# Two decoder blocks on one core: every projection with the tokens stationary, and strips turned by a trip through device memory

## The chip, the cores and the metric

The kernel runs on one core of a Trainium2 chip. The metric is device time in microseconds, from one execution of the whole program. Three runs of the kernel before gave 2118.93, 2119.08 and 2119.95 us; the median, 2119.08 us, is the time before. The profile is of one further execution, whose span from first to last instruction is 2117.7 us.

Engine names in the rows: PE is TensorE's matmuls, PEld its loads of the stationary operand, DVE is VectorE, ACT is ScalarE, POOL is GpSimd, SP is SyncE, whose queue (SPq) issues most DMAs.

## The reference

256 tokens of 2048 features go through two blocks, in float32.

```python
# block one
a = rms_norm(h, norm_mix)
q, k, v = split(a @ sb_w_qkv)                     # 16 heads of 128
A = exp(log_sigmoid(z) + sum of -softplus(z) of the keys between)   # z = q k / sqrt(128), keys before the query
h = h + (A @ v) @ sb_w_o
h = h + square(relu(rms_norm(h, norm_mlp) @ mlp_w1)) @ mlp_w2      # 8192 hidden
x = rms_norm(h, final_norm)
# block two
z = rms_norm(x, pre_mix_g) @ w_in                 # q, k, v: 8 heads of 128; u: 1024 for the pool
a = softmax attention over chunks, with a bias by distance
p = (trailing means of u over 2, 4, 8, 16 tokens, less u) @ pool_w, per group of 256, times pool_scale
x = x + rms_norm(concat(a, p) @ w_o, post_mix_g)
up = causal_dwconv(rms_norm(x, pre_ffn_g) @ w_up)  # 3 taps over tokens, 2 x 5632
y = (gelu(up[:, :5632]) * up[:, 5632:]) @ w_down
out = x + rms_norm(y, post_ffn_g)
```

## The kernel before

**Pieces and strips.** The program is one list of 746 pieces. A piece is 256 rows by 512 columns of some weight matrix (512 KB); 8, 10 or 12 pieces make a strip of 512 output columns. Each weight and each activation is split into a high half, rounded for the fast float32 matmul (fp32r), and the rest as a low half; a product is high x high + high x low + low x high. The split of piece i is an ACT copy into `Wh` (L930) and a DVE subtraction into `Wl` (L1146). There are 6 raw buffers (`NRAW`) and 5 split buffers (`NW`), and the split of piece i+4 stands in the program ahead of PE's products of piece i.

**Two kinds of piece.** In kind "N" the tokens are stationary (`row_products`, 12 matmuls of 512 columns) and the result has tokens as partitions, in two banks of PSUM. In kind "T" the weights are stationary and the tokens, high and low side by side, are moving:

```python
for m in range(4):
    c = slice(t * 512 + m * 128, t * 512 + (m + 1) * 128)
    mm(P[:, m, :], wh[:, c], x, ...)                  # 512 columns: x high and x low
    r = mm(P[:, m, 0:TOK], wl[:, c], x[:, 0:TOK], ...)  # 256 columns
```

That is 8 matmuls of 512 columns and 8 of 256 a piece; the result has features as partitions, in four banks, and its two halves have to be added. What needs features as partitions is of kind T: q and k of both attentions, w1 of the MLP, the pool's u, and w_up. These are 52 strips of 8 pieces, 416 pieces. v, w_o, w2 and w_down are of kind N, 328 pieces. Two pieces of `pool_w` have a kind of their own with the columns of T.

**Evacuation of a T strip.** ACT copies the low half (`low_copy`, L900), DVE adds it to the high half (`low_add`, L1104) into `T1`. For q and k DVE scales by the norm's factor, which lies as a row over all partitions (`r_a`, `r_b`; L1201); for w_up and the pool POOL does it (L1482, L1464); for w1 DVE squares (L1272), ACT and DVE make the halves (L1020, L1275). The factor gets into a row by a `spread`: a diagonal matrix on DVE (L1121), a float32 matmul with ones, a copy on ACT (L982).

**PSUM.** There are two sets of four banks. Strips use them in turn, and side work (scores, weights, values, norms, turned tiles) uses the set that the running strip does not (`side_set`).

**Order.** `plan_program` walks through the pieces. For each it emits the splits that are due, the products, at a strip's last piece the evacuation, and then the jobs that were put down for this piece by `after(i, job)` and `later(n, job)`. Each engine gets its part of the steps in that one order, and waits only on semaphores. So a job's place says behind which split and before which split each engine meets it. With v the first piece of a group's v strip, the scores come after piece v+1, the attention weights after v+8, the values after v+12.

**Trips through device memory** exist for eight strips of rows: after w_o of block one, after the last w2 strips and once for w_up. SP writes the rows (L856, two DMAs of 256 KB), waits for them, reads them back in four DMAs of 128 KB as 32-token blocks (L861), and DVE transposes 32x32 blocks (L1242). The softmax's probabilities take a similar trip (L865, L868, L1339).

Of the kernel before, what the change touches and what calls it, by code (L numbers as in the profile page):

```python
# [4 lines left out]
F32 = mybir.dt.float32  # L5
# [47 lines left out]
def plan_program(sem):  # L53
    p = Plan(sem)
    step, done, after, later = p.step, p.done, p.after, p.later
    free = {n: [] for n in ("QK1", "T0", "T1", "E", "zs", "set0", "set1", "mT", "qk0", "qk1", "v0", "v1", "A0", "A1")}
# [3 lines left out]
    def side_set():  # L60
        return 1 - now[0]
# [13 lines left out]
    tile_hl = [None] * KT  # L75

# [7 lines left out]
    def strip(w, col, ks, mov, tiles, evac, kind="T", koff=0):  # L84
        first = len(p.pieces)
        for n, kp in enumerate(ks):
            src = (w, "rows", kp * 256, col)
            p.pieces.append(dict(src=src, shape=2, mov=mov, kt=2 * (kp - koff), tiles=tiles, kind=kind, first=n == 0,
                                 last=n == len(ks) - 1, evac=evac, wide=False, early=None))
        return first  # L90
# [12 lines left out]
    def rms(name, col):  # L103
# [3 lines left out]
        r, diag = done("rms_r"), done("rms_diag")  # L107
        step("rms", set=s, col=col, need=st["total"], free=list(free[f"set{s}"]), ones=ones0, ident=ident,
             total=total, mean=mean, root=root, rec=rec, sq=sq, prod=prod, r=r, diag=diag)
        free["zs"], free[f"set{s}"] = [total], [mean]  # L110
        st[name + "c"] = r
        st["diag"] = diag
# [8 lines left out]
    def row_norm(squared=False, spreads=None):  # L121
# [3 lines left out]
        kw = dict(square=done("rms_r")) if squared else dict(square=None)  # L125
        if spreads:
            kw.update(diag=done("rms_diag"), ident=ident, zs_free=list(free["zs"]))
        step("row_norm", need=st["rows_sq"], total=total, mean=mean, root=root, rec=rec, sq=sq, prod=prod, r=r, spreads=spreads, **kw)
        if squared:
            st["r2sq"] = kw["square"]  # L130
        if spreads:
            st["diag"] = kw["diag"]
            after(p.at + 2, lambda: spread(spreads, "r_b"), ahead=True)

    def row_pair():
# [5 lines left out]
        both, diag = done("rms_r"), done("rms_diag")  # L141
        step("row_pair", need=st["rows_sq"], zs_free=list(free["zs"]), ident=ident, total=total, mean=mean, first=first,
             square=square, moved=moved, mean2=mean2, second=second, both=both, diag=diag)
# [185 lines left out]
    for c, n in enumerate((6, 5, 5)):  # L329
        for j in range(n):  # L330
# [3 lines left out]
            if j == 0:  # L334
                p.pieces[i]["wide"] = True
# [1406 lines left out]
```

## Time and profile before

| | |
|---|---|
| median of 3 runs | 2119.08 us |
| span of the profiled execution | 2117.7 us (the median is 1.4 us above it) |
| PE busy | 2110.5 us, 10990 matmul records |
| PEld busy | 1810.4 us |
| DVE busy | 1259.2 us (59%) |
| ACT busy | 1049.5 us (50%) |
| POOL busy | 189.2 us (9%) |
| DMA | 415.11 MB, 61.3% of 16 engines on SP's queue |

Matmuls overlap in the records, so a mean of 390 ns is the life of one matmul, from its start to its end; what a stream of them costs is read from start to start. A float32 matmul that is not of the fast kind shows as two records.

### The profile page before, as it was taken

The numbers are of one execution on the slowest core, as the hardware profiler recorded it, in microseconds if no ns is written. First come the engines' busy times: TensorE is split into PE (matmuls) and PEld (weight loads), VectorE is DVE, ScalarE is ACT, GpSimd is POOL, SyncE is SP. The second block draws the span as 40 slices with busy tenths as digits, with TensorE's granted clock in tenths as the row PEclk, the third lists the DMA queues.
The fourth block names the chain that finished last, engine by engine and source line by source line (L and its number), as shares of the span: only waits on it lengthen the run. The fifth ranks groups of instructions, "written<-read, shape, count | busy, mean of one in ns | idle before, by whom it ended". The sixth has DMA issues, their size and how long they took to land.

```text
span 2117.7 us, 26776 instructions
## 1 busy us (share of the span) xinstructions
PE 2110.5 (100%) x10990; PEld 1810.4 (85%) x10990; DVE 1259.2 (59%) x1341; ACT 1049.5 (50%) x1222; POOL 189.2 (9%) x90
## 2 busy tenths in 40 slices
PE   9999999999999999999999999999999999999998
PEld 8888888888888888888888888888888888888887
DVE  6555656656455555465667755576666644566565
ACT  7554555544334443344555635465455443455543
POOL 3000000000000000000004000002222100222210
PEclk9999999999999999999999999999999999999999
DMA  8565557765666666666676567655655666556663
GB/s 289 171 207 172 180 169 232 223 195 174 209 193 183 199 211 191 186 193 195 219 238 189 178 210 228 195 183 173 195 191 178 217 191 192 182 175 199 204 210 120
DMA packets 220363, 415.11 MB, mean 196 GB/s; under 512 B 13521, under 2 KB 23889, under 8 KB 219729
## 3 DMA queue, kind: packets, MB, share of 16 engines
q1 hardware_dynamic: 219376, 408.92, 61.3%
q10 hardware_dynamic: 864, 4.49, 0.6%
q8 instruction: 86, 1.41, 0.3%
q14 instruction: 37, 0.30, 0.0%
HBM read 405.49 MB, written 7.86 MB: 195 GB/s over the span
## 4 chain that ended last, share of the span: by engine, by line
PE 100%; ACT 0%; DVE 0%; issue 0%; POOL 0%; DVEq 0%; POOLq 0%
PE ps L1503 99%; PE ps L1506 0%; ACT T L1075 0%; DVE QK L1390 0%; ACT raw L1088 0%; ACT aHL L954 0%; ACT zs L1085 0%; DVE rs L1407 0%; POOL ones L1434 0%; ACT rs L1080 0%; POOL ident L1432 0%; DVE rs L1404 0%; DVE rs L1409 0%; DVE rs L1399 0%; POOL tri L1433 0%
## 5 line engine op out<-in xcount | busy, mean ns | idle before, releaser
L1146 DVE TENSOR_TENSOR Wl<-raw,Wh 128x1024 fp32r<-128x1024 f32 x743 | 911.8, 1246 | 640.6 <-ACT Wh L930 639.9
L1503 PE MATMUL ps<-aHL,Wh 128*128 128x512 f32 x3336 | 1158.7, 392 | 0.5 <-ACT aHL L954 0.4
L930 ACT ACTIVATE Wh<-raw 128x1024 fp32r<-128x1024 f32 x743 | 767.6, 1054 | 588.9 <-PE ps L1503 585.4
L1503 PE MATMUL ps<-aHL,Wl 128*128 128x256 f32 x3328 | 929.3, 279 | 0.0
L1503 PEld LDWEIGHTS ps<-aHL,Wh 128*128 128x128 f32 x3336 | 624.2, 187 | 139.5 <-issue 0.9
L1503 PEld LDWEIGHTS ps<-aHL,Wl 128*128 128x128 f32 x3328 | 628.2, 189 | 0.5
L1503 PE MATMUL ps<-Wh,hid 128*128 128x512 f32 x1728 | 533.1, 389 | 0.0
L1503 PEld LDWEIGHTS ps<-Wh,hid 128*128 128x128 f32 x1728 | 324.4, 188 | 67.5
L1503 PE MATMUL ps<-Wl,hid 128*128 128x512 f32 x864 | 336.2, 389 | 0.0
L1503 PEld LDWEIGHTS ps<-Wl,hid 128*128 128x128 f32 x864 | 162.2, 188 | 33.5
L1503 PE MATMUL ps<-Wh,oHL 128*128 128x512 f32 x512 | 158.7, 389 | 0.0
L1482 POOL TENSOR_TENSOR T<-T,r_b 128x1024 f32<-128x1024 f32 x22 | 71.2, 3235 | 645.4 <-DVE T L1104 391.1
L1503 PE MATMUL ps<-Wh,aHL 128*128 128x512 f32 x384 | 121.1, 391 | 0.0
L1503 PEld LDWEIGHTS ps<-Wh,oHL 128*128 128x128 f32 x512 | 96.1, 188 | 20.1
L1503 PE MATMUL ps<-Wl,oHL 128*128 128x512 f32 x256 | 99.6, 389 | 0.0
L1104 DVE TENSOR_TENSOR T<-ps,T 128x1024 f32<-128x1024 f32 x54 | 66.0, 1223 | 54.8 <-ACT T L900 54.8
L900 ACT ACTIVATE T<-ps 128x1024 f32<-128x1024 f32 x54 | 55.3, 1024 | 69.1 <-PE ps L1503 69.1
L1503 PEld LDWEIGHTS ps<-Wh,aHL 128*128 128x128 f32 x384 | 72.1, 188 | 15.0
L1464 POOL TENSOR_TENSOR E<-T,r_b 128x1024 f32<-128x1024 f32 x2 | 7.0, 3486 | 825.7 <-DVE T L1104 813.2
L1503 PE MATMUL ps<-Wl,aHL 128*128 128x512 f32 x192 | 74.7, 389 | 0.0
L1486 POOL TENSOR_TENSOR E<-E,zs 128x1024 f32<-128x1024 f32 x11 | 49.0, 4455 | 95.6 <-DVE E L1366 95.6
L1503 PEld LDWEIGHTS ps<-Wl,oHL 128*128 128x128 f32 x256 | 48.1, 188 | 9.7
(175 smaller groups left out, 792.2 us busy)
## 6 DMA issues: line engine op xcount, KB each, us to landing
raw<-in_mlp_w_dram SPq DMA_DIRECT2D x256, 512.0 KB, 4.3
raw<-in_w_up_dram SPq DMA_DIRECT2D x176, 512.0 KB, 3.9
raw<-in_sb_w_qkv_dram SPq DMA_DIRECT2D x93, 512.0 KB, 4.8
raw<-in_w_down_dram SPq DMA_DIRECT2D x88, 512.0 KB, 4.2
raw<-in_w_in_dram SPq DMA_DIRECT2D x64, 512.0 KB, 4.4
raw<-in_sb_w_o_dram SPq DMA_DIRECT2D x32, 512.0 KB, 5.3
raw<-in_w_o_dram SPq DMA_DIRECT2D x32, 512.0 KB, 4.3
passed_rows<-xN SPq DMA_DIRECT2D x16, 256.0 KB, 4.3
```

The source lines that it names most:

```text
L900: e.activation(T0[:, :, :], ps[st["set"]][:, :, TOK:2 * TOK], ACT.Copy).then_inc(st["copied"][0], 1)
L930: e.activation(Wh[:, i % NW, :], rawv[:, i % NRAW, :], ACT.Copy).then_inc(st["hi"][0], 1)
L1104: e.tensor_tensor(T1[:, :, :], ps[st["set"]][:, :, 0:TOK], T0[:, :, :], ALU.add).then_inc(st["summed"][0], 1)
L1146: e.tensor_tensor(Wl[:, i % NW, :], rawv[:, i % NRAW, :], Wh[:, i % NW, :].bitcast(F32), ALU.subtract).then_inc(st["lo"][0], 1)
L1464: e.tensor_tensor(E4, T1[:, :, :], rows4("r_b"), ALU.mult).then_inc(st["scaled"][0], 1)
L1482: e.tensor_tensor(T1[:, :, :], T1[:, :, :], rows4("r_b"), ALU.mult).then_inc(st["done"][0], 1)
L1486: e.tensor_tensor(E4, E4, Z4, ALU.mult).then_inc(st["done"][0], 1)
L1503: return e.matmul(o, l, r, start=start, stop=stop, skip_group_check=True)
```

## The change

- Every projection piece but the two of the pool is of kind "N". A strip takes two banks of PSUM. Sets 0 and 1 have two banks each and are used by the strips in turn; set 2 has four banks and is the side set, and the pool pieces use it too.
- A strip that needs features as partitions makes a trip. ACT copies its two banks to `T0` with the norm's factor as a scale per partition (tokens are partitions now), or with relu and then a square (`stage_rows`). SP writes `T0` out as two DMAs; two pieces later it waits for them and reads back as four (`land_rows`); two pieces after that DVE transposes the 32x32 blocks into the place wanted (`turn_strip`). One trip is under way at a time; another waits in a list. Columns within each group of 128 of these weights are permuted on the host to fit the blocks.
- Low copies, sums and scalings of such strips go, and with them `spread`, `diagonal`, `r_a`, `r_b`, and the matmul on `r_a` that opened four strips.
- Scores, attention weights and values stand three pieces later (v+4, v+11, v+15), for the first group two more.
- The strips of w_o in both blocks and of w_down are paired: with a tail of 2, the first pair's strips run all but their last two pieces, then these.
- At the conv, both halves of the older taps stand one piece after the newest, the gate one later, its halves two later.

The core of the diff (lines of the planner, then of the engines):

```diff
     def side_set():
-        return 1 - now[0]
+        return 2
...
+    def strip_pair(w, s4, ks, tail, mov, tiles, evacs, koff=0):
+        first, n = len(p.pieces), len(ks) - tail
+        for i in range(2):
+            strip(w, (s4 + i) * STRIP, ks, mov, tiles, evacs[i], koff)
+        a, b = p.pieces[first:first + len(ks)], p.pieces[first + len(ks):]
+        p.pieces[first:] = a[:n] + b[:n] + a[n:] + b[n:]
         return first
...
+    def trip(s, k, n, how, col, need, landed_to):
+
+        if st.get("landing"):
+            st["landing"].append(lambda: trip(s, k, n, how, col, need, landed_to))
+            return
+        st["landing"] = [lambda: landed_to(moved)]
...
+        step("stage_rows", n=n, set=s, mm=k, how=how, col=col, need=need, t0_free=list(free["T0"]), staged=staged, squared=squared,
+             passed=passed, held=st.get(("trip", n % 2)))
...
+        def back():
+            step("land_rows", n=n, passed=passed, done=moved)
+            later(2, landed)
...
+        later(2, back)
...
     for g in range(4):
-        after(first["v", g] + 1, sb_scores(g))
-        after(first["v", g] + 8, sb_weights(g))
-        after(first["v", g] + 12, values(g, 1))
+        at = first["v", g] + (0 if g else 2)
+        after(at + 4, sb_scores(g))
+        after(at + 11, sb_weights(g))
+        after(at + 15, values(g, 1))
...
-    for s4 in range(4):
-        strip("sb_w_o", s4 * STRIP, ALL8, "oHL1", oHL_tiles, evac_rows(s4, "mlp"), kind="N")
+    for s4 in (0, 2):
+        strip_pair("sb_w_o", s4, ALL8, 0 if s4 else 2, "oHL1", oHL_tiles, [evac_rows(s4, "mlp"), evac_rows(s4 + 1, "mlp")])
...
-            summed, kw = common(s, k, free["T1"])
-            squared = done("relu_squared")
-            hi, lo = done("hid_hi"), done("hid_lo")
-            step("relu", t0=t0, squared=squared, hi=hi, lo=lo, **kw)
-            free["T0"], free["T1"] = [lo], [squared]
-            hid_tiles[t0:t0 + 4] = [lo] * 4
+            def landed(moved):
+                turned, hi, lo = done("hid_turned"), done("hid_hi"), done("hid_lo")
+                step("turn_strip", to="T1", need=[moved, *free["T1"]], done=turned)
+                step("hid_halves", t0=t0, need=turned, hi=hi, lo=lo)
+                free["T0"], free["T1"] = [turned], [lo]
+                hid_tiles[t0:t0 + 4] = [lo] * 4
+            trip(s, k, n, "relu", None, [], landed)
...
-        ps = [ctx.enter_context(nc.psum_tensor(f"ps{i}", [128, 4, 512], F32)) for i in range(2)]
+        ps = [ctx.enter_context(nc.psum_tensor(f"ps{i}", [128, n, 512], F32)) for i, n in enumerate((2, 2, 4))]
...
+                elif k == "stage_rows":
+                    if st["held"]:
+                        e.wait_ge(*st["held"])
+                    for t in range(2):
+                        e.wait_ge(*(st["squared"] or st["staged"])[t])
+                        e.dma_start(passed_strip[st["n"] % 2, t * 128:(t + 1) * 128, :], strip_rows[:, t, :]).then_inc(st["passed"][0], 16)
+                elif k == "land_rows":
+                    e.wait_ge(*st["passed"])
+                    for a in range(4):
+                        e.dma_start(strip_landed[a * 32:(a + 1) * 32, :, :],
+                                    passed_strip[st["n"] % 2].rearrange("(c j) (a f) -> a j c f", c=8, a=4)[a]).then_inc(st["done"][0], 16)
...
+                elif k == "stage_rows":
+                    for t in st["need"] + st["t0_free"]:
+                        e.wait_ge(*t)
+                    for t in range(2):
+                        e.wait_ge(*st["mm"][t])
+                        if st["how"] == "relu":
+                            e.activation(strip_rows[:, t, :], ps[st["set"]][:, t, :], ACT.Relu).then_inc(st["staged"][t][0], 1)
+                        else:
+                            e.activation(strip_rows[:, t, :], ps[st["set"]][:, t, :], ACT.Copy,
+                                         scale=cols[st["col"]][:, t:t + 1]).then_inc(st["staged"][t][0], 1)
...
+                    e.transpose(dst, strip_blocks).then_inc(st["done"][0], 1)
```

How the order of the instructions moves is seen at three places. The first is PE at the start of the second group of w1 strips, behind the last w2 strip of the first. Before (`hid` are the hidden tiles, stationary; `aHL` the normed input):

```order
L1503 MATMUL ps<-Wh,hid 128x512 x2
L1503 MATMUL ps<-Wl,hid 128x512
L1503 MATMUL ps<-Wh,hid 128x512
L1503 MATMUL ps<-r_a,ones 128x256 [waits s_row_copied,s_w_lo,s_rows_added]
L1503 MATMUL ps<-aHL,Wh 128x512
L1503 MATMUL ps<-aHL,Wl 128x256
L1503 MATMUL ps<-aHL,Wh 128x512
L1503 MATMUL ps<-aHL,Wl 128x256
```

Now:

```order
L1538 MATMUL ps<-Wh,hid 128x512 x2
L1538 MATMUL ps<-Wl,hid 128x512
L1538 MATMUL ps<-Wh,hid 128x512
L1538 MATMUL ps<-Wh,aHL 128x512 [waits s_w_lo,s_rows_added]
L1538 MATMUL ps<-Wl,aHL 128x512
L1538 MATMUL ps<-Wh,aHL 128x512 x2
L1538 MATMUL ps<-Wl,aHL 128x512
L1538 MATMUL ps<-Wh,aHL 128x512 x2
L1538 MATMUL ps<-Wl,aHL 128x512
```

The matmul on `r_a` is gone, and the pairs of 512 and 256 columns have become triples of 512.

The second is ACT from the first k strip's copy to the first scores. In the change, L1036 is the copy of a strip's two banks to `T0`, L978 the split of a weight piece, L1054 the copy of the scores:

```order
L978 ACTIVATE Wh<-raw 128x1024 [waits s_mm,s_raw3]
L1036 ACTIVATE T<-ps,rs 128x512 [waits s_mm_row0,s_qk_turned,s_rms_r]
L1036 ACTIVATE T<-ps,rs 128x512 [waits s_mm]
L978 ACTIVATE Wh<-raw 128x1024 [waits s_mm,s_raw4]
L978 ACTIVATE Wh<-raw 128x1024 [waits s_mm,s_raw5]
L978 ACTIVATE Wh<-raw 128x1024 [waits s_mm,s_raw0]
L978 ACTIVATE Wh<-raw 128x1024 [waits s_mm,s_raw1]
L978 ACTIVATE Wh<-raw 128x1024 [waits s_mm,s_raw2]
```

The copy of the k strip waits until the q strip is turned, and the splits of later pieces stand behind it. DVE's transposes stand four splits apart, the later one a single split ahead of the scores' softplus:

```order
L1196 TENSOR_TENSOR Wl<-raw,Wh 128x1024 [waits s_w_hi] x4
L1248 STREAM_TRANSPOSE QK<-T 128x1024 [waits s_strip_moved]
L1196 TENSOR_TENSOR Wl<-raw,Wh 128x1024 [waits s_w_hi] x4
L1248 STREAM_TRANSPOSE QK<-T 128x1024 [waits s_strip_moved]
L1196 TENSOR_TENSOR Wl<-raw,Wh 128x1024 [waits s_w_hi]
L1251 SCALAR_TENSOR_TENSOR E<-zs,E 128x1536 [waits s_sb_act]
```

In their place before stood a sum (L1104) and a scaling (L1201) for each strip, with no wait on a DMA.

The third is SP at the first two trips, where before there were only loads of weights (L930 in the change):

```order
L930 DMA raw<-in_sb_w_qkv_dram 128x2x512 [waits s_w_lo] x17
L905 DMA passed_strip<-T 128x512 [waits s_rows_staged] x2
L930 DMA raw<-in_sb_w_qkv_dram 128x2x512 [waits s_w_lo] x2
L909 DMA T<-passed_strip 32x8x128 [waits s_strip_passed]
L909 DMA T<-passed_strip 32x8x128 x3
L930 DMA raw<-in_sb_w_qkv_dram 128x2x512 [waits s_w_lo] x2
L905 DMA passed_strip<-T 128x512 [waits s_rows_staged] x2
```

Two loads stand between a strip's writes and its reads; the reads wait in SP's line for the writes to land, ahead of the next loads.

## Rows read from the trace of the kernel before

**Rows 1.** The page, part 1: busy time, share of the span, instructions.
```profile
span 2117.7 us, 26776 instructions
PE 2110.5 (100%) x10990; PEld 1810.4 (85%) x10990; DVE 1259.2 (59%) x1341; ACT 1049.5 (50%) x1222; POOL 189.2 (9%) x90
```

**Rows 2.** The chain that ended last, in time: start us, us, what.
```profile
6.06 1095.12 PE ps L1503 x5628
...
1377.81 0.48 ACT aHL L954
```

**Rows 3.** Timeline, PE, a T stretch: start us, us of one, engine, line, operation, tiles.
```profile
440.04 0.39 PE L1503 MATMUL ps<-aHL,Wh 128*128 128x512 f32 x1
...
519.78 0.39 PE L1503 MATMUL ps<-aHL,Wh 128*128 128x512 f32 x1
```

**Rows 4.** Timeline, PE, an N stretch: the matmul on the low weights.
```profile
540.14 0.39 PE L1503 MATMUL ps<-Wl,hid 128*128 128x512 f32 x1
...
620.38 0.39 PE L1503 MATMUL ps<-Wl,hid 128*128 128x512 f32 x1
```

**Rows 5.** Stretches: length, busy (x records) by engine, granted clock, DMA share, GB/s.
```profile
440.00:520.00 80.00, 80.00 (x463) 70.54 (x462) 46.80 (x39) 36.42 (x36) 0.00 (x0) 1.00 0.64 198
540.00:620.00 80.00, 80.00 (x355) 66.24 (x354) 39.31 (x36) 31.02 (x30) 0.00 (x0) 1.00 0.64 195
323.00:397.00 74.00, 74.00 (x340) 61.73 (x339) 45.77 (x50) 38.01 (x55) 0.00 (x0) 1.00 0.73 234
0.00:50.00 50.00, 48.58 (x272) 42.84 (x273) 34.67 (x46) 34.36 (x50) 16.26 (x20) 1.00 0.86 296
```

**Rows 6.** Groups by shape, PE: count, busy us, mean ns of one, idle before.
```profile
L1503 PE MATMUL ps<-Wh,aHL 128*128 128x512 f32 x384 | 121.1, 391 | 0.0
```

**Rows 7.** Timeline, PE, where a strip opens with the matmul on r_a.
```profile
652.11 0.59 PE L1503 MATMUL ps<-r_a,ones 128*128 128x256 f32 x2
652.35 0.59 PE L1503 MATMUL ps<-aHL,Wh 128*128 128x512 f32 x1
652.78 0.28 PE L1503 MATMUL ps<-aHL,Wl 128*128 128x256 f32 x1
```

**Rows 8.** Groups by shape, ACT and DVE: what a trip adds and what goes.
```profile
L991 ACT ACTIVATE vb<-ps,rs 128x512 f32<-128x512 f32 x12 | 7.7, 678 | 1.8 <-PE ps L1503 1.8
L942 ACT ACTIVATE T<-xN 128x512 f32<-128x512 f32 x32 | 19.9, 626 | 23.7 <-DVE xN L1229 8.0 <-DVE xN L1238 7.8 <-DVE xN L1232 7.8
L1242 DVE STREAM_TRANSPOSE T<-E 128x1024 f32<-128x1024 f32 x8 | 10.0, 1245 | 6.8 <-DMA E<-passed_rows 6.6
L1104 DVE TENSOR_TENSOR T<-ps,T 128x1024 f32<-128x1024 f32 x54 | 66.0, 1223 | 54.8 <-ACT T L900 54.8
```

**Rows 9.** Timeline, a trip: SP's issues and DVE's transpose; then SP's of another.
```profile
344.91 0.94 SPq L856 DMA_DIRECT2D passed_rows<-xN  x2
351.04 2.62 SPq L861 DMA_DIRECT2D E<-passed_rows  x4
356.00 1.25 DVE L1242 STREAM_TRANSPOSE T<-E 128x1024 f32<-128x1024 f32 x1 [0.83 <-DMA E<-passed_rows]
...
1015.72 0.94 SPq L856 DMA_DIRECT2D passed_rows<-xN  x2
1020.52 1.80 SPq L861 DMA_DIRECT2D E<-passed_rows  x4
```

**Rows 10.** Waits of SP's queue: us in total, times, longest us.
```profile
SPq L882 <- DVE Wl L1146: 1696.9, 706, 12.0
```

**Rows 11.** Timeline, the first norm: PE's sums, DVE's step behind the finished column.
```profile
45.40 0.50 PE L1503 MATMUL ps<-ones,zs 128*128 128x1 f32 x4
...
47.15 0.42 DVE L1121 TENSOR_TENSOR zs<-ident,rs 128x256 f32<-128x256 f32 x1
```

**Rows 12.** Timeline, POOL, the second pool strip's windows: the scaling and the last step.
```profile
1141.29 3.17 POOL L1464 TENSOR_TENSOR E<-T,r_b 128x1024 f32<-128x1024 f32 x1 [12.46 <-issue]
...
1157.23 1.19 POOL L1475 COPY QK<-QK 128x16 f32<-128x16 f32 x1
```

More of the change, by code:

```diff
@@ L179, in r_job, with landed @@
-    def r_job(name, col, row):
-        def f():
-            rms(name, col)
-            after(p.at + 1, lambda: spread(name, row), ahead=True)
-        return f
+    def trip(s, k, n, how, col, need, landed_to):
+        if st.get("landing"):
+            st["landing"].append(lambda: trip(s, k, n, how, col, need, landed_to))
+            return
+        st["landing"] = [lambda: landed_to(moved)]
+        staged = [done("rows_staged") for t in range(2)]
+        squared = [done("rows_squared_up") for t in range(2)] if how == "relu" else None
+        passed, moved = done("strip_passed", 32), done("strip_moved", 4 * 16)
+        step("stage_rows", n=n, set=s, mm=k, how=how, col=col, need=need, t0_free=list(free["T0"]), staged=staged, squared=squared,
+             passed=passed, held=st.get(("trip", n % 2)))
+        st["trip", n % 2] = moved
+        free[f"set{s}"] = [staged[1]]
+        free["T0"] = [moved]
+        def back():
+            step("land_rows", n=n, passed=passed, done=moved)
+            later(2, landed)
+        def landed():
+            first, *others = st["landing"]
+            st["landing"] = []
+            first()
+            for job in others:
+                job()
+        later(2, back)
@@ L354, in evac_pool, with landed @@
     def evac_pool(u):
+        n = next_trip()
         def f(s, k):
-            summed, kw = common(s, k, free["T1"])
-            step("sum", **kw)
-            def windows():
-                scaled = done("win_scaled")
+            def landed(moved):
+                turned = done("win_turned")
+                step("turn_strip", to="E", need=[moved, *free["E"]], done=turned)
+                free["T0"] = [turned]
                 rounds = []
@@ L376, in means @@
                 free["E"], free["qk1"] = [h[1][1]], [h[1][1]]
-            windows()
+            trip(s, k, n, "copy", "b", [st["r4c"]], landed)
         return f
@@ L683, in plan_program @@
         need = []
-        if q["first"]:
+        if q["kind"] == "P":
+            need += free["set2"]
+        elif q["first"]:
             now[0] = 1 - now[0]
+            set_of[q["strip"]] = now[0]
             need += free[f"set{now[0]}"]
@@ L1669, in tensor_program @@
                 elif k == "mixed_norm":
+                    for t in st["free"]:
+                        e.wait_ge(*t)
                     for n in range(14):
```

322 lines of the change are left out of this document (149 added, 173 removed).

## Prediction

> **What bounds the kernel now.** I read the page's first part first. [Rows 1]: PE is busy for 2110.5 of 2117.7 us; DVE for 59% and ACT for 50%. Busy is not the same as streaming, so next the chain that ended last: 99% of it is line 1503, the matmuls. In order of time its first long link is 1095 us of nothing but PE, and the one wait between PE's links, at 1377.8 us on a copy by ACT, is under 1 us long [rows 2]. So nothing that DVE, ACT, POOL or a DMA does sets the time today, apart from that wait and the two ends. A change can win only by what PE's own instructions cost, and it can lose by making PE wait for the first time.
>
> What does one piece (256 rows of weights by 512 columns) cost on PE? Both kinds stream 6144 columns. A feature piece does it in 8 matmuls of 512 columns and 8 of 256; a token piece does it in 12 of 512. In the timeline, a feature stretch starts a pair at 440.04 us and another at 519.78 [rows 3]. The neighbouring starts are 0.34 to 0.35 us apart, so these are 230 pairs of 0.3467 us, and a feature piece costs 8 x 0.3467 = 2.774 us. In a token stretch the matmul on the low weights comes once in three: 540.14 to 620.38 us are 118 triples of 0.680 us [rows 4], so a token piece costs 4 x 0.680 = **2.720 us**. The granted clock is 1.00 in both stretches [rows 5], the 2.4 GHz level, where 512 columns take 213.3 ns. The token matmul's slot is 226.7 ns, so 13 ns are left for each matmul; 346.7 less 320 ns leaves the same 13 ns for each of a feature pair. Equal columns, four instructions fewer: that is the 0.054 us. The kernel already runs such pieces with the same kind of stationary tile in the v strips (ps<-Wh,aHL, 384 records of 391 ns [rows 6]; the first record of rows 3, of the other kind, lives 0.39 us too).
>
> The Trainium skill, "TensorE: Matmul & The Clock Gate", section "Wait — 56ns, not 53.3ns?", gives a warm matmul's fixed cost as about 2.5 ns beyond its columns. Here the row shows 13 ns and decides. By the page's figure the four matmuls of a piece would be worth 10 ns, and 416 pieces 4.2 us.
>
> **The sum on PE.** All 416 feature pieces become token pieces: 416 x 0.0536 = **22.3 us less**. The spreads go (three: zs,ones) and so do the four matmuls on r_a that opened a strip, seven places in all. The place at 652 us shows the price [rows 7]: the two records take 652.11 to 652.35, and the next matmul's slot is 0.43 us where its neighbours' is 0.23. That is 0.24 + 0.20 = 0.44 us, and 7 x 0.44 = **3.1 us less**. The two pool pieces stay feature pieces. The attention's own matmuls and the turned tiles stay as they are.
>
> **What every strip gains elsewhere: a trip.** Two ACT copies of 128x512 (like L991, 0.68 us each [rows 8]; with relu two squares more, 0.63 by L942), two DMAs out, four DMAs back in 128 KB parts, one 32x32 block transpose on DVE (L1242, 1.25 us). Against them stand the removed low copy on ACT, the sum on DVE (1.22) and the scaling on DVE or POOL (3.2 us, [rows 12]). DVE and ACT loads hardly move and are hidden at 59% and 50%. What counts is **how long a trip takes and who stands in line behind it**. The kernel before makes eight such trips for the w_o and last w2 rows. One of them in full [rows 9]: out from 344.91, second write issued at 345.51, reads issued from 351.04 to 353.66, transpose at 356.00: 10.5 us from the second write. The part out takes 5.5 us here; at 1016 us, in a quieter stretch, it takes 4.2 from the second write.
>
> Let 0 be the end of a strip on PE. The copies end at about 0.7 (row 0 is copied earlier, at its own semaphore; relu ends at 2). The data are back at 0.8 + 10.5 = 11.3, with relu at 12.6, and turned at 12.6 to 13.9.
> - *DVE* comes to the transpose's wait after its split for piece +8, which needs PE's piece +3 done: 3 x 2.72 + 1.05 + 1.25 = 10.5. It stands 1 to 2 us. Behind it waits the split of piece +9, which PE wants at 8 x 2.72 = 21.8. Turn, low half and split are 3.7 us, so the data may land as late as 18.1. This is the cover of all 52 trips, some 6 us deep.
> - *ACT* at the high half waits for the transpose with the same splits behind it; its part is inside that sum.
> - *SP* issues the reads after the writes have landed, two pieces later in its order, with the loads of weights behind. Of the span, SP waits 1696.9 us for a buffer to come free [rows 10], so it reaches the wait late anyway; the loads are six pieces ahead.
> - *The DMA engines*: a trip adds 1 MB to the 4 MB of weights that a strip loads. Quiet stretches use 0.64 of the engines; 323 to 397 us, where four trips run beside four strips, has just this mix and uses 0.73, with PE busy throughout (rows x340 over 74.00 us of 74.00; [rows 5]). Cost 0.
> - *Hidden halves*: the last w1 strip's tiles are made about 16 us after its end. The w2 strip wants them 8 or 10 pieces on, at 21.8 or 27.2. Cost 0. For w_o and w_down the pairing of strips moves the want back further.
> - *Scores*: they moved from v+1 to v+4 in the order, so PE reaches them 5 x 2.72 = 13.6 us after the end of k, with q and k turned at 12.6. They fit by 1 us. The distances from there to the weights (7 pieces) and values (4) are the same as before; a piece is shorter only in the q strip. Cost 0.
> - *The first scores* are the exception. The first q strip may not be copied until r1 exists, after piece 13, and k's copy waits until q is turned, since both use T0. PE's sums for the norm stand at 45.40 and the column is ready when DVE starts the diagonal at 47.15; with one small step more, 47.3 [rows 11], so 1.9 us after piece 13. Two copies: 3.3. Back 8.3 to 10.5 later (out 4.2 to 5.5, reads issued over 1.8 to 2.6, 2.3 until the transpose; [rows 9]), turned at 12.9 to 15.1. In PE's count, with 4 pieces and the sums' 0.36 between, that is 1.7 to 3.9 us after piece 17. Then the same for k: copies 1.3, back 8.3 to 10.5, turned 1.25, so 12.6 to 17.0 after piece 17, and PE is there after five pieces, at 13.6. PE waits between 0 and 3.4 us; I take **1.5 us more**, near the middle of the late half.
> - POOL loses 24 scalings of 3.2 us. No gain: nothing waits for it on the chain. Its last window round begins 12.6 us after strip u1 and takes 13.9 (1144.5, where the scaling ends, to 1158.4), ending at 26.5 [rows 12]; DVE comes to the means after 11 pieces, at 30. Hidden by 3 us.
>
> Sum on the profiled execution: 2117.7 - 22.3 - 3.1 + 1.5 = 2093.8 us of span. The median of the runs is 1.4 us above this span, so I forecast **2095.2 us**. It is 1.1% faster. A measurement here can tell about 0.2% (4.2 us) from no change.
>
> [...]
>
> **Rivals.**
> 1. *PE waits at the tight places.* For: the scores fit by 1 us only, in six groups, and the first w_up strips and the pool depend on several trips in a row. Against: the eight trips of before cost PE nothing. If each scores step waited 1.5 us (a trip of 13 us) and one other place 2 us, it would be 10 us more: about 2105 us. Chance 0.14.
> 2. *The fixed cost per matmul is not what goes.* If the pieces won only 4.2 us, the time would be 2117.7 - 4.2 - 3.1 + 1.5 + 1.4 = 2113.3 us; if nothing, 2117.5. This is the Trainium skill's 2.5 ns, named above. Against: the v strips' 0.680 us triples. Chance 0.04, half of it within 0.2%.
> 3. *Slower: a trip outlasts the cover.* Place: DVE at the transpose, with the weight splits behind it and PE at the wait for the low weights. Point from which it decides: data back later than 18.1 us after the strip. Price: 52 trips times what is beyond. 0.5 us beyond in each eats the whole gain of 24; data back at 18.7 gives 2095 + 52 x 0.6 = 2126 us. For: the reads queue behind 512 KB loads on the same queue. Against: it takes 7 us more than any trip seen, and in the stretch with the same mix the four trips were turned in time and PE never waited. Chance 0.05.
> 4. *The change does not do what it says*, because some strips are still paced by loads, as at the start, where DMA share is 0.86 [rows 5]: then the first 16 pieces win nothing, 0.9 us. It is inside the range.
>
> **How the numbers follow.** The forecast has 0.77, rival 1 0.14, rival 2 0.04, rival 3 0.05. Lower end: no wait at the first scores gives 2093.7, and the 0.7 us wait before w_up (the turned tiles get banks of their own) with some of the smaller gaps may go as well: 2092. Upper end: 3.4 us at the first scores gives 2097, and most of rival 1 goes to 2106. Range 2092 to 2106. Faster by over 0.2%: 0.77 + 0.14 + half of rival 2 = 0.92; within: 0.03; slower: 0.05.
>
> **What would show it.** In the profile of the changed kernel, feature strips' triples start 0.680 us apart; PE has about 9340 records instead of 10990; DMA share rises by about 0.08; the transposes start 10.5 to 12 us after their strip; DVE's wait for passed rows is 50 to 150 us in all, without any of PE; one PE wait of 1 to 3 us stands before the first scores near 66 us. The forecast is wrong if the triples are longer than 0.680 us in strips with a trip beside them, or if PE waits for the low weights after each strip.

## The result and the profile after

The kernel after the change takes **2264.44 us** (median of 4 runs, 2255.01 to 2265.32) where the kernel before takes 2119.09 (2118.93 to 2119.95): ratio 1.067, interval 1.0655 to 1.0693. It is 6.7% slower; 2095.2 was forecast. The profiled execution has a span of 2263.6 us, 145.9 more than before.

The page's first part and its chain, of the kernel after (compare [rows 1] and [rows 2]):

```profile
span 2263.6 us, 23747 instructions
PE 2175.9 (96%) x9304; PEld 1750.4 (77%) x9304; DVE 1221.2 (54%) x1312; ACT 1072.6 (47%) x1303; POOL 121.5 (5%) x66
PE 69%; DMA 12%; DVE 9%; ACT 4%; SPq 2%; POOL 2%; issue 2%; ACTq 0%; POOLq 0%; DVEq 0%
```

PE has 1686 records fewer, as meant, and yet is busy for 65 us more. Before, all but 7.2 us of the span was PE; now PE is idle for 87.7 us. The chain, 99% PE before, runs for almost a third of the span through other engines, 12% of it through DMAs, nearly all of them those of trips. So there are two separate effects: **PE is slower while it runs**, and **it waits**.

*The pace.* A triple is three matmuls, one of them on the low weights; a slot is the time from one matmul's start to the next. In a quiet stretch of w1, PE's timeline has 191 triples without a gap between these two rows (start us, length us; compare [rows 4]):

```profile
410.98 0.39 PE L1538 MATMUL ps<-Wl,aHL 128*128 128x512 f32 x1
...
544.67 0.40 PE L1538 MATMUL ps<-Wl,aHL 128*128 128x512 f32 x1
```

133.69 / 191 = 0.700 us for a triple, not 0.680: a slot of 233.3 ns in place of 226.7. The granted clock is 1.00 there. The w2 strips, whose pieces the change does not touch, have the same 0.700 (191 triples from 545.38 to 679.08). So a token piece costs 2.800 us here. Later strips run down to 232.4 ns; over the whole trace, neighbouring starts without a gap are 232.9 ns apart in the mean. That is 6.2 ns more in each of 744 x 12 = 8928 matmuls, **55 us** beyond the forecast (59.5 if every piece cost 2.800).

*The waits*, of the kernel after (engine line <- engine tile line: us in total, times, longest; compare [rows 10]):

```profile
PE ps L1538 <- DVE Wl L1196: 66.1, 25, 6.0
PE ps L1538 <- DVE QK L1248: 12.8, 6, 5.6
DVE T L1248 <- DMA T<-passed_strip: 207.3, 38, 11.6
SPq L909 <- DMA passed_strip<-T: 71.8, 34, 5.9
SPq L930 <- DVE Wl L1196: 1573.0, 629, 13.4
```

PE waits for low weights, and DVE, which makes them, has stood at the transpose of a trip. Summed over PE's starts, what is beyond a slot comes to 123 us (8.7 before): 97 in the 22 w_up strips (from 1440 us), 19 in the attentions, and almost nothing in w1's 16 strips, though each of them makes a trip too.

One w_up trip in full, of the timeline of the kernel after: ACT's copies, then SP's queue, DVE, ACT and PE:

```profile
1492.51 1.24 ACT L1036 ACTIVATE T<-ps,rs 128x512 f32<-128x512 f32 x2
...
1479.81 18.17 SPq L930 DMA_DIRECT2D raw<-in_w_up_dram  x6
1498.07 0.89 SPq L905 DMA_DIRECT2D passed_strip<-T  x2
1503.36 1.52 SPq L930 DMA_DIRECT2D raw<-in_w_up_dram  x2
1504.92 1.95 SPq L909 DMA_DIRECT2D T<-passed_strip  x4
...
1494.09 3.49 DVE L1196 TENSOR_TENSOR Wl<-raw,Wh 128x1024 fp32r<-128x1024 f32 x3
...
1514.18 1.25 DVE L1248 STREAM_TRANSPOSE T<-T 128x1024 f32<-128x1024 f32 x1 [7.44 <-DMA T<-passed_strip]
...
1515.46 2.07 ACT L1117 ACTIVATE zs<-T,conv 128x256 f32<-128x256 f32 x4 [10.73 <-DVE T L1248]
1517.44 1.99 ACT L978 ACTIVATE Wh<-raw 128x1024 fp32r<-128x1024 f32 x2
...
1518.51 1.23 DVE L1196 TENSOR_TENSOR Wl<-raw,Wh 128x1024 fp32r<-128x1024 f32 x1 [3.09 <-ACT Wh L978]
...
1514.88 0.39 PE L1538 MATMUL ps<-Wh,aHL 128*128 128x512 f32 x1
1519.89 0.77 PE L1538 MATMUL ps<-Wh,aHL 128*128 128x512 f32 x1 [4.61 <-DVE Wl L1196]
```

The copies end at 1493.75, but the write starts at 1498.07: SP is in a load whose buffer DVE frees with the last of the three splits that end at 1497.58. The reads again come after two loads. The data are back at 1514.18, 20.4 us after the copies. Behind the transpose stand ACT's four conv copies, ACT's high half, then DVE's low half: 5.71 us until PE starts again.

What PE does then, of the kernel after's windows (stretch, length, busy and count of PE, PEld, DVE, ACT, POOL, granted clock, DMA share, GB/s):

```profile
1512.00:1516.00 4.00, 3.27 (x15) 2.32 (x13) 1.25 (x1) 0.54 (x2) 0.00 (x0) 1.00 0.66 199
1516.00:1520.00 4.00, 0.11 (x1) 0.14 (x1) 1.49 (x2) 3.43 (x6) 0.00 (x0) 0.95 0.00 0
1520.00:1522.00 2.00, 2.00 (x5) 1.61 (x6) 2.00 (x6) 0.00 (x0) 0.00 (x0) 0.50 0.44 109
...
1524.00:1526.00 2.00, 2.00 (x10) 1.61 (x9) 1.06 (x2) 2.00 (x3) 0.00 (x0) 1.00 0.38 65
```

After 4.61 us of idle PE the granted clock is 0.50, the 1.2 GHz level, while PE works again, and each slot nearly doubles. It is back at 1.00 by 1524. So this wait costs 4.6 us of idleness, and seven slots then take 3.12 us (1519.89 to 1523.01) where 1.63 are due: 1.5 us more. The trace has sixteen such stretches before its last 10 us, each beside a wait of PE of 1.9 to 6.0 us; a wait of 2.9 us that ends at 152.4 us has none. PE works at 0.50 for 59 us of them, half of which, 30 us, is lost.

The difference of the spans, 145.9 us, is then: -25.4 (the pieces' 22.3 and the rows' 3.1, as forecast) + 55 (pace) + 80.5 (PE's idle time, 87.7 less 7.2), which leaves 36. The slots at the lower clock account for 30 of them; the mean granted clock, 0.984 where it was 0.999, allows 0.015 x 2263.6 = 34 at most. Some 6 us stay unassigned.

### The profile page after: what moved, and what is told of

It is laid out like the page before. It is cut to its first block, busy times and chain, and to the rows that moved or that the text cites. A ratio compares the mean times of both kernels' runs of the same rounds, so it can differ in the third digit from the quotient of the medians.

```text
span 2263.6 us, 23747 instructions
## 1 busy us (share of the span) xinstructions
PE 2175.9 (96%) x9304; PEld 1750.4 (77%) x9304; DVE 1221.2 (54%) x1312; ACT 1072.6 (47%) x1303; POOL 121.5 (5%) x66
## 4 chain that ended last, share of the span: by engine, by line
PE 69%; DMA 12%; DVE 9%; ACT 4%; SPq 2%; POOL 2%; issue 2%; ACTq 0%; POOLq 0%; DVEq 0%
PE ps L1538 69%; DMA T<-passed_strip 7%; DMA passed_strip<-T 5%; DVE Wl L1196 4%; SPq L909 2%; POOL E L1521 2%; ACT Wh L978 2%; DVE E L1408 1%; DVE zs L1408 1%; DVE T L1248 1%; ACT zs L1117 1%; ACT E L1117 1%; DVE QK L1248 0%; SPq L930 0%; DVE hid L1414 0%
## 5 line engine op out<-in xcount | busy, mean ns | idle before, releaser
L1538 PE MATMUL ps<-Wh,aHL 128*128 128x512 f32 x3712 | 1191.0, 400 | 51.4 <-DVE Wl L1196 50.5
L978 ACT ACTIVATE Wh<-raw 128x1024 fp32r<-128x1024 f32 x743 | 764.2, 1054 | 556.0 <-PE ps L1538 552.8
L1538 PEld LDWEIGHTS ps<-Wh,aHL 128*128 128x128 f32 x3712 | 707.3, 191 | 229.9 <-issue 51.7
L1538 PE MATMUL ps<-Wl,aHL 128*128 128x512 f32 x1856 | 739.9, 399 | 0.0
L1538 PE MATMUL ps<-Wh,hid 128*128 128x512 f32 x1728 | 548.6, 398 | 15.6 <-DVE Wl L1196 15.6
L1538 PEld LDWEIGHTS ps<-Wl,aHL 128*128 128x128 f32 x1856 | 354.5, 191 | 82.8
L1248 DVE STREAM_TRANSPOSE T<-T 128x1024 f32<-128x1024 f32 x38 | 47.3, 1245 | 207.3 <-DMA T<-passed_strip 207.3
L1117 ACT ACTIVATE E<-T,conv 128x256 f32<-128x256 f32 x44 | 22.9, 590 | 114.8 <-DVE T L1248 114.8
L1117 ACT ACTIVATE zs<-T,conv 128x256 f32<-128x256 f32 x44 | 22.8, 589 | 100.5 <-DVE T L1248 100.5
L1076 ACT ACTIVATE hid<-T 128x1024 fp32r<-128x1024 f32 x16 | 17.0, 1062 | 97.4 <-DVE T L1248 97.4
L1036 ACT ACTIVATE T<-ps,rs 128x512 f32<-128x512 f32 x72 | 46.4, 678 | 18.6 <-PE ps L1538 11.6
```

The source lines that it names most:

```text
L978: e.activation(Wh[:, i % NW, :], rawv[:, i % NRAW, :], ACT.Copy).then_inc(st["hi"][0], 1)
L1036: e.activation(strip_rows[:, t, :], ps[st["set"]][:, t, :], ACT.Copy, scale=cols[st["col"]][:, t:t + 1]).then_inc(st["staged"][t][0], 1)
L1076: e.activation(hid1[:, st["t0"]:st["t0"] + 4, 0:TOK], T1[:, :, :], ACT.Copy).then_inc(st["hi"][0], 1)
L1117: e.activation(C[:, m, :], T1[:, m, :], ACT.Identity, scale=conv[:, 2, n0 + m:n0 + m + 1], bias=conv[:, 3, n0 + m:n0 + m + 1]).then_inc(st ...
L1248: e.transpose(dst, strip_blocks).then_inc(st["done"][0], 1)
L1538: return e.matmul(o, l, r, start=start, stop=stop, skip_group_check=True)
```

## The experiments

Two questions: what makes PE's slot longer (e1, e2, e3, e10, e11), and what makes PE wait (e4 to e9, e12).

### The pace: addresses in SBUF

In the compiled kernel before, `Wh` lies at byte 73856 of each partition, 128 beyond a multiple of 256, and so do `aHL` (142208) and `hid` (174976). The change removes `r_a` and `r_b` (2048 bytes) and puts `rs2` (128 bytes) in their place, and `aHL` (140288) and `hid` (173056) now lie on multiples of 256. The other suspect was PSUM, where a strip now has two banks in a new set.

**e1_pad1920**: the kernel after, with all 1920 bytes put back.

```diff
         conv = sb("conv", [128, 4, 88])
+        sb("pad", [128, 480])
         rs = sb("rs", [128, 24])
```

> The changed kernel with 1920 bytes a partition left free where r_a, r_b and their neighbours lay, so that every tile behind them (the input tiles, the hidden tiles) has the address it had in the kernel before. Theory A (a token matmul's slot grew from 226.7 to 233.3 ns because the stationary tiles moved against the weights' tiles in SBUF): slots of 226.7 ns again, 744 pieces x 0.08 us = 60 us less, about 2200 to 2210 us, with the waits of PE in the w_up strips about as they are or a little longer. Rival A2 (the slot grew because all strips now use PSUM banks 0 to 3, or for want of the other kind of piece): no change, 2264 us within 5.

Measured 2225.72 us (2222.60 to 2230.62), ratio to the kernel before 1.050 [1.0479, 1.0518]; the slot is 226.7 ns.

**e2_pad128**: the same with `[128, 32]`, so 128 bytes.

> The changed kernel with only 128 bytes a partition left free at the same place. Theory A, if what counts is the address in steps of 256 bytes (input tiles at 142208 = 128 beyond a multiple of 256 before, at 140288 = a multiple of 256 in the change, weights at 128 beyond one in both): slots of 226.7 ns, 2200 to 2210 us. Theory A with another rule than this (512 bytes, or the distance itself): a slot between or at 233.3. Rival A2: 233.3 ns, 2264 us.

Measured 2225.81 us (one run). From the first of these rows to the last are 351 triples without a gap, of w2 and w1 strips:

```profile
555.07 0.40 PE L1539 MATMUL ps<-Wl,hid 128*128 128x512 f32 x1
...
793.76 0.39 PE L1539 MATMUL ps<-Wl,hid 128*128 128x512 f32 x1
```

238.69 / 351 / 3 = 226.7 ns. 128 bytes bring the whole slot back. Yet the gain in e1 and e2 is 38.7 us, not 55, and both end above the 2200 to 2210 expected: the strips are shorter and the trips are not, so the waits grow (in e1 PE is idle for 101.1 us, 13.4 more).

**e3_before_shift**: the kernel before, with the same 128 bytes ahead of `rs`.

> The kernel before, with 128 bytes a partition left free ahead of the small tiles, so that the input and hidden tiles start at a multiple of 256 bytes. Theory A in steps of 256 bytes: token pieces go from 2.72 to 2.80 us (328 pieces: 26 us), feature pieces by something of the kind (the same two tiles are read, the roles exchanged: up to 416 x 0.08 = 33 us): 2145 to 2180 us. Rival A2: 2119 us, within 3.

Measured 2155.76 us (one run), 36.7 more than before, with the old banks and no more waiting. Its timeline, from the first row to the last 191 triples of a w2 strip:

```profile
530.24 0.40 PE L1504 MATMUL ps<-Wl,hid 128*128 128x512 f32 x1
...
663.40 0.39 PE L1504 MATMUL ps<-Wl,hid 128*128 128x512 f32 x1
```

133.16 / 191 / 3 = 232.4 ns. The banks are out: 128 bytes of address do it, in a kernel that the change never touched.

**e10_weights_moved** and **e11_both_moved** ask which address. They start from the kernel with all three changes (e5, below), in which `Wh`, `aHL` and `hid` all lie 128 beyond a multiple. e10 takes its padding out and puts it ahead of `Wh`; e11 keeps it and puts another there.

```diff
+        sb("pad", [128, 32])
         Wh = sb("Wh", [128, NW, 1024], F32R)
...
         conv = sb("conv", [128, 4, 88])
-        sb("pad", [128, 32])
         rs = sb("rs", [128, 24])
```

> The kernel with all three changes, but its 128 bytes of padding stand ahead of the weights Wh and Wl instead of behind them: Wh then lies on a multiple of 256 bytes, aHL where it was (128 beyond a multiple of 256). Every other order is unchanged. Theory C, that the distance between the moving tile and the stationary tile decides (equal remainders of 256 are fast): they differ again, the slot of a token matmul is 232 to 233 ns and the time about 2150 us (2107.8 and the 43 us between the two kernels that differ by 128 bytes and have the later turns). Rival C2, that only the stationary tile's own address decides (128 beyond a multiple of 256 is fast): 226.7 ns and 2108 us. Rival C3, that any of the two on a multiple of 256 makes it slow: 232 to 233 ns and 2150 us too; the next kernel tells it from C.

> The kernel with all three changes, and 128 more bytes ahead of the weights: Wh, Wl, aHL, hid and oHL all lie on multiples of 256 bytes. Theory C (equal remainders are fast): the slot is 226.7 ns and the time 2108 us. Rivals C2 (the stationary tile on a multiple of 256 is slow) and C3 (any of the two on a multiple is slow): 232 to 233 ns and about 2150 us.

e10: 2148.92 us (both runs), ratio 1.0137 [1.0116, 1.0157]. e11: 2095.17 and 2102.76 us, ratio 0.990 [0.988, 0.9922]. A w_up stretch of 371 triples in each, e10's first:

```profile
1411.08 0.39 PE L1540 MATMUL ps<-Wl,aHL 128*128 128x512 f32 x1
...
1669.72 0.40 PE L1540 MATMUL ps<-Wl,aHL 128*128 128x512 f32 x1
```

```profile
1374.04 0.40 PE L1541 MATMUL ps<-Wl,aHL 128*128 128x512 f32 x1
...
1626.33 0.39 PE L1541 MATMUL ps<-Wl,aHL 128*128 128x512 f32 x1
```

258.64 / 371 / 3 = 232.4 ns and 252.29 / 371 / 3 = 226.7 ns. By (address of weights, address of tokens) modulo 256: (128, 128) and (0, 0) give the short slot, (128, 0) and (0, 128) the long one. Equal remainders decide, not a certain address of one tile (C, not C2 or C3). e11 came out some 9 us under the 2108 expected: its order is e5's, its slot too, but in the profiled run it has nearly none of e5's waits. Why is not shown.

### The waits: what stands around a trip

**e4_turn_later**: in the kernel after, the transposes of w1's and w_up's strips come four pieces after the reads, not two.

```diff
             step("land_rows", n=n, passed=passed, done=moved)
-            later(2, landed)
+            later(4 if to_hid else 2, landed)
...
-            trip(s, k, n, "relu", None, [], landed)
+            trip(s, k, n, "relu", None, [], landed, True)
...
-                trip(s, k, n, "copy", "b", [st["r6"]], landed)
+                trip(s, k, n, "copy", "b", [st["r6"]], landed, True)
```

> The changed kernel with the transpose and all behind it two pieces later in the order for the w1 and w_up strips (landed four pieces after the reads' place instead of two). Theory B (in the w_up strips DVE and ACT stand at the transpose's wait, and behind it the splits, the taps of the conv and four copies come too late for PE; the data land 12 to 16 us after the second write, so two pieces more would let them pass): PE's waits in w_up go nearly all, some 85 us less, about 2180 us, DVE's wait for the strips back falls from 258 us in all to under 80, slots stay 233.3 ns. Rival B2 (the DMA engines: loads of weights come late because the trips take their share): PE waits as before, 2264 us within 15, since nothing is taken from the DMAs. Rival B3 (POOL's gate and the halves behind it hold ACT): under a third of the gain.

Measured 2166.24 us (2161.84 to 2171.71), ratio 1.022 [1.0202, 1.0241]: 98 us less. DVE's waits for strips put into T fall from 207.3 to 45.2 us, and w_up's 97 us beyond the slots to 7. So PE's waits depend on where the transpose stands in DVE's order. The slot is still long, 232.4 ns, now in the w1 and w2 strips too.

**e6_pad_and_later**: e2 and e4 together.

> The changed kernel with the 128 bytes left free and the transposes of w1 and w_up two pieces later; the attentions as in the change. Theories A and B add up: 2166 less 744 x 0.08 = 60 gives 2106 us; with the attentions' waits (about 17 us in the run with the later transposes) and a few us of waits in w_up that shorter pieces bring back, 2106 to 2116 us. Rival: the waits in w_up grow as the pieces get shorter, as they did by some 20 us when the pace alone was mended, so 2120 to 2130 us.

Measured 2123.37 us (10 runs, 2118.52 to 2130.05), ratio 1.002 [1.0008, 1.003]: both repaired bring it back to the kernel before, and the gains nearly add up. The 2106 to 2116 expected took 60 us off e4 for the pace; but e4's slot is 232.4 ns, so it was worth 8928 x 5.7 ns = 51, and the profiled runs of the two differ by 48.9. The time lies in the rival's range, without the rival's reason: the waits in w_up did not grow. PE still has some 30 to 35 us beyond its slots, over half of it in the attentions.

**e5_all_three**: e6, with the trips of q and k also four pieces after the reads except the pool's, and the jobs of the attentions (scores, weights, values, for the first group four pieces) and the mixed norm two later. (The scaling of v in block two then also waits for the addition of the bias, whose PSUM set it would otherwise meet.)

```diff
     for g in range(4):
-        at = first["v", g] + (0 if g else 2)
+        at = first["v", g] + (2 if g else 6)
...
-        after(first2["v", g] + 4, sm_scores(g))
-        after(first2["v", g] + 13, sm_turn(g))
-        after(first2["v", g] + 15, values(g, 2))
+        after(first2["v", g] + 6, sm_scores(g))
+        after(first2["v", g] + 15, sm_turn(g))
+        after(first2["v", g] + 17, values(g, 2))
...
-    after(first2["o"] + 8, mixed_row)
+    after(first2["o"] + 10, mixed_row)
```

> The changed kernel with the 128 bytes left free (slots of 226.7 ns), the transposes of w1 and w_up strips two pieces later, and in both attentions the transposes of q and k two pieces later too, with scores, weights and values two pieces later (four in the first group, where two trips follow one another). If theories A and B and the waits at the scores are all that stood against the forecast, the kernel runs as forecast for the change: 2093 to 2105 us, PE's waits under 12 us in all. Rival: with shorter pieces the trips come late again somewhere (they are as long as before, a piece is 0.08 us shorter, so a strip 0.64): 2110 to 2125 us, the waits left in w_up.

Measured 2107.75 us (2104.68 to 2108.71), ratio 0.994 [0.9925, 0.9955]. It is 0.6% faster than the kernel before, and just above the 2093 to 2105 expected. 21.4 us beyond the slots are left, of which 14 are waits in w_up.

**e7_taps_apart**: the kernel after, in which the older taps of the conv (DVE, 8 steps, 3.2 us) no longer stand in one block behind the transpose.

```diff
                 later(1, lambda: older(u, c, 0))
-                later(1, lambda: older(u, c, 2))
-                later(2, lambda: gated(st["older", which]))
+                later(2, lambda: older(u, c, 2))
+                later(3, lambda: gated(st["older", which]))
```

> The changed kernel with the older taps of the conv in two steps a piece apart and the gate one later, as in the kernel before; nothing else. Theory B says that DVE's eight tap steps (3.2 us) and ACT's four copies (2.1 us) stand between the transpose and the next splits of weights, so four of the eight out of the way let one split pass 1.6 us earlier, in 22 strips: 20 to 45 us less than 2264. Rival B4 (only the landing of the strip counts, not what stands behind it): within 8 us of 2264.

Measured 2224.22 us (one run), 40 less.

**e8_writes_by_act**: the kernel after, the two writes of a trip issued by ACT right behind its copies (the first lines below are SP's, the last ACT's; the `dma_start` moves with them).

```diff
-                elif k == "stage_rows":
-                    if st["held"]:
-                        e.wait_ge(*st["held"])
-                    for t in range(2):
-                        e.wait_ge(*(st["squared"] or st["staged"])[t])
...
                             e.activation(strip_rows[:, t, :], strip_rows[:, t, :], ACT.Square).then_inc(st["squared"][t][0], 1)
+                    if st["held"]:
+                        e.wait_ge(*st["held"])
+                    for t in range(2):
+                        e.wait_ge(*(st["squared"] or st["staged"])[t])
```

> The changed kernel with the two writes of a strip issued by ACT right after its copies, on ACT's own queue, instead of by SP behind the next load of weights. If a trip is long because its writes wait in SP's line and ring, the reads are issued 1 to 2 us earlier in w_up and PE waits less, 20 to 50 us off 2264. If the reads' place in SP's order (behind the loads that wait for splits) or their landing sets the trip's length, within 10 us of 2264; ACT's own issue time may even cost some.

Measured 2263.66 us (one run): nothing is won. The same place of its timeline shows why:

```profile
1492.36 1.48 ACTq L1040 DMA_DIRECT2D passed_strip<-T  x2
...
1502.45 1.50 SPq L924 DMA_DIRECT2D raw<-in_w_up_dram  x2
1504.00 1.95 SPq L903 DMA_DIRECT2D T<-passed_strip  x4
```

The write goes out at once, and the reads still stand on SP behind two loads: 11.6 us from write to read, in every second strip. The run did not clear SP; it moved the same wait one step on.

**e12_trip_by_act**: so both ends by ACT (`land_rows` moves too; its edit is like e8's).

> The kernel after the change, but both ends of a strip's trip (the two writes and the four reads) are issued by ACT's queue at the same places of the order, so they no longer stand behind SP's loads of weights, which wait for a buffer. Read from the trace of the kernel after: in every second w_up strip the first write is issued 4.3 us after the copies end, in the others 0.8 us, and the transpose starts 19 to 20.5 us after the copies in the first and 13 us in the others; with the writes alone by ACT nothing was won, since the reads then stood 11.6 us after the write. Theory: SP's order is a part of the trip. Then the long trips become like the short ones (12 to 14 us after the copies), each odd w_up strip's wait of 4 to 6 us mostly goes, and the time is 2200 to 2235 us; ACT spends about 2 us more a trip on issuing, which is hidden. Rival: the trip is long because the transfers themselves are slow beside the loads, or what stands behind the transpose is all that matters: 2255 to 2270 us.

Measured 2176.98 us (2 runs, 2176.51 and 2177.45), ratio 1.027 [1.0238, 1.0298]: **87 us less**, well below the 2200 to 2235 expected. Its waits and one trip, of the timeline:

```profile
PE ps L1537 <- DVE Wl L1195: 15.3, 15, 3.9
DVE T L1247 <- DMA T<-passed_strip: 43.9, 25, 5.2
```

```profile
1476.76 1.24 ACT L1025 ACTIVATE T<-ps,rs 128x512 f32<-128x512 f32 x2
1477.52 1.66 ACTq L1035 DMA_DIRECT2D passed_strip<-T  x2
...
1485.16 1.04 ACTq L1039 DMA_DIRECT2D T<-passed_strip  x2
...
1490.90 1.24 DVE L1247 STREAM_TRANSPOSE T<-T 128x1024 f32<-128x1024 f32 x1
```

From the end of the copies (1478.00) to the transpose it is 12.9 us, and 11.8 to 13.1 in the eleven trips from 1460 to 1710 us. DVE comes to the transpose shown straight from a split, so the data were back by then. In the kernel after it is 13 us in one strip and 19.1 to 20.6 in the next, by turns. Of the 6.6 us between the two kinds, 3.5 are the write's wait in SP's order (4.3 us behind the copies, not 0.8), and 2.1 lie behind the issue of the last read: 6.4 us to the transpose in the long trips, 4.3 in the short ones, 4.8 here. So SP's order is over half of what made the trips late, and all of it goes with SP's queue; why the reads of a long trip also take longer to land is not shown.

**e9_all_and_taps**: e5 with e7's edit.

> This is the kernel of the run with all three changes (2107.75 us, of which PE waits 21.4 us where the kernel before waits 8.8), and the older taps of w_up's strips no longer come in one block: the second half of the taps one piece later, the gate one piece later again. By the theory that the steps behind the transpose are part of what makes PE wait, the waits in w_up (about 9 us between 1360 and 1664 us and 4 to 6 us between 1924 and 2016 us) shrink to a few us and those of the attentions stay: 2098 to 2104 us. By the rival that there the length of the trip itself or the loads decide, nothing changes: 2107 to 2108 us. If the gate now comes too late for the halves, PE waits for the w_down strips instead and it is slower than 2108.

Measured **2094.40 us** (2093.91 to 2094.83), ratio 0.988 [0.9864, 0.9897]: 1.2% faster than the kernel before, the best version here, and below the 2098 to 2104 expected. Of its page, its windows, its waits and its timeline (370 triples from 1374.64 to 1626.24):

```profile
span 2092.1 us, 23749 instructions
PE 2083.7 (100%) x9304; PEld 1728.7 (83%) x9304; DVE 1235.8 (59%) x1312; ACT 1081.3 (52%) x1303; POOL 117.0 (6%) x66
```

```profile
1374.00:1626.00 252.00, 252.00 (x1113) 208.66 (x1112) 170.02 (x203) 144.39 (x188) 24.00 (x5) 1.00 0.81 241
```

```profile
DVE T L1250 <- DMA T<-passed_strip: 9.8, 10, 2.6
```

```profile
1374.64 0.39 PE L1540 MATMUL ps<-Wl,aHL 128*128 128x512 f32 x1
...
1626.24 0.39 PE L1540 MATMUL ps<-Wl,aHL 128*128 128x512 f32 x1
```

251.60 / 370 = 0.680 us, through the first half of the strips that waited 97 us, with the DMA engines at 0.81. SP still issues every trip here. Most writes now go out 2.2 to 2.4 us behind the copies (4.0 in e5), and most transposes start 15.1 to 16.3 us behind them, in odd and even strips alike, which their later place covers. How much of the 13 us under e5 the taps bring is open: e11, which has e5's taps and was run beside e9, took 2095.17 and 2102.76 us.

## Why the prediction was wrong

The mechanism of the gain was right, and two steps failed: the pace of a piece was taken over from the old trace, and SP's queue and the work behind a landing were put at nothing or too low. Both of the signs of being wrong that the prediction names came: triples longer than 0.680 us, and PE waiting for the low weights (behind most w_up strips, not behind w1's).

- **"A token piece costs 4 x 0.680 = 2.720 us"** is the mis-sized term: 2.79 to 2.80 in the kernel after, about 55 us in all. The number was read rightly and carries over only if weights and tokens keep equal remainders. The change frees `r_a` and `r_b`, and the prediction never asked what their 2048 bytes held in place. Neither did any rival.
- **416 x 0.0536 = 22.3 and 7 x 0.44 = 3.1 us less** were right once the addresses were. 2117.7 - 22.3 - 3.1 = 2092.3, without the first scores' 1.5, and e9's span is 2092.1, with 8.4 us of idle PE where the kernel before has 7.2. PE has 9304 records (9340 forecast).
- **"so it reaches the wait late anyway; the loads are six pieces ahead"** (SP, put at nothing) is the step that failed for the waits. It argued that SP's long waits for a buffer [rows 10] come before the trip's anyway. But SP waits for a split, the split stands on DVE behind a transpose and the taps, and the transpose waits for the trip's reads, which stand on SP: a ring. In every second w_up strip a load holds the write by 4.3 us and the reads with it. e12 takes the trip out of that queue and 87 us go.
- **"10.5 us from the second write"**, taken from w_o's trips [rows 9], was the time of a trip with no load of weights between its writes and its reads. In the w_up strips it is 10.7 to 16.0 us, 15.6 in the one shown, and the data are back there at 21.7 us after the strip's end (the copies end 1.3 us behind it).
- **"the data may land as late as 18.1. This is the cover of all 52 trips"**: worked out for w1. Its 3.7 us of work behind the landing are a turn, a low half and a split; ACT's high half was said to be inside that sum, but the split waits for it too. In the first w1 strip the turn starts at 447.25 and the split ends at 451.95, 4.7 us later; the data come early enough there, so nothing waits. In w_up it is 5.71 us, with ACT's four conv copies ahead of the high half of the next weights, and the older taps behind the next split: the cover is 2 us thinner, and e7, which only spreads the taps, wins 40 us. Without those, 21.7 us against 18.1 would still have been too late: rival 3's point was right and its chance of 0.05 was not. Its price, landing beyond the cover for all 52 trips, was of the wrong shape: 22 strips pay nearly all.
- **The first scores, 1.5 us.** The transpose of k starts at 77.53 us, 12.6 after the copies end, where 8.3 to 10.5 were allowed, and PE waits 5.55 us, where at most 3.4 was allowed. With the trips on ACT's queue it is 3.2 us beyond the slots (e12). The row of PE:

```profile
78.88 1.41 PE L1538 MATMUL ps<-QK 128*128 128x128 f32 x5 [5.55 <-DVE QK L1248]
```

- **"They fit by 1 us"** (the other groups' scores, cost 0) failed in the same way: about 11 us beyond the slots in the other groups' places. Rival 1 had this at 10 us, with the right mechanism.
- **What a wait costs.** All prices counted a wait as its idle time. The lower clock behind it adds 30 us here, a fifth of the loss.
- **DMA engines, cost 0**, stands: e9 shows 0.81 of them busy over 252 us without a wait of PE. Rival 2 fell: beyond its columns a matmul costs 13 ns with equal remainders and 19 to 20 with unequal. The Trainium skill's 2.5 ns ("TensorE: Matmul & The Clock Gate", section "Wait — 56ns, not 53.3ns?") was seen in no run here.
- **The chances.** 0.77 + 0.14 + half of 0.04 is 0.93, not 0.92; nothing hangs on it.

Open: why the slow slot is 232.4 ns in some stretches and 233.3 in others of the same addresses (in the w1 strips 233.3 in the kernel after and 232.4 in e4); how much of e5's gain over e6 each of its delays brings; and e9 with the trips issued by ACT, which was not tried. Offsets other than 0 and 128 modulo 256 were not tried either.

## What to carry to other kernels

Before a term is taken over from the old trace, ask whether what it depends on moves: here freeing two small buffers moved the big ones by 1920 bytes and cost about 6 ns in each of 8928 matmuls. Of the placements tried, those with the two tiles of a matmul at equal remainders modulo 256 bytes were the fast ones; padding gets them there. Compare the addresses before and after, and look at the slot in a stretch that the change should not touch.

Where a chain leaves an engine and comes back through a queue that also carries the loads, follow it round: the queue's head can wait for an engine that waits for something further back in the queue, and here that made every second trip of w_up late. Issue the trip from another queue, or put its end later in the order and spread the work behind it. Moving half of it (e8) won nothing.

## What was unexpected of the hardware

- 128 bytes of padding change the slot of a 512-column fp32r matmul from 226.7 to 232.4 or 233.3 ns, by whether moving and stationary tile have equal remainders modulo 256 (all four combinations of 0 and 128). In the kernel before it is worth 36.7 us of 2119.
- After PE had been idle for 4.61 us the granted clock stood at 0.50, the 1.2 GHz level, for the first microseconds of work, and was 1.00 again within 5 us of PE's restart.
